# A MoE decoder layer in fp32: experts' rows gathered from an fp32 copy, and a scatter among the last down products

## What is computed

```python
logits = (xt @ router_w + router_b)
top_val, top_idx = lax.top_k(logits, 4)
gates = softmax(top_val)
# for each expert e, over the rows xb of its tokens with gates wb:
gu = xb @ w_gate_up[e] + b_gate_up[e]          # 1024 -> 2048
g, u = gu[:, :1024], gu[:, 1024:]
g = min(g, 7); u = clip(u, -7, 7)
act = (u + 1) * (g * sigmoid(1.702 * g))
ys = (act @ w_down[e] + b_down[e]) * wb        # 1024 -> 1024
# summed back into the tokens' rows, plus the residual
```

## Time and profile before

| | |
|---|---|
| median of 3 runs | 1109.57 us |
| profiled execution | 1112.72 us |
| its span | 1110.9 us |
| PE (matmul) busy | 1056.3 us, 95% |
| DVE, ACT busy | 282.3 us, 157.9 us |
| HBM read | 430.82 MB, 389 GB/s over the span |
| mean granted TensorE clock | 0.985 of full |

### The profile page before, as it was taken

How to read it: one execution, slowest core, us unless ns; L and a number is a source line. 1 busy time by engine, 2 the same in 40 slices (tenths; PEclk the granted TensorE clock), 3 DMA queues, 4 the chain that set the end, 5 groups by cost and what they waited for, 6 DMA issues and landing times.

```text
span 1110.9 us, 14806 instructions
## 1 busy us (share of the span) xinstructions
PE 1056.3 (95%) x6243; PEld 489.1 (44%) x6243; DVE 282.3 (25%) x719; ACT 157.9 (14%) x325; POOL 29.8 (3%) x32
## 2 busy tenths in 40 slices
PE   9999999999999999979999979899798898999998
PEld 7788885543333333333333333333233333333333
DVE  2599843531111111111111111111011111111131
ACT  3453351410000000000000000000000000000011
POOL 1000053000000000000000000000000000000000
PEclk9999999999999999999999989999899999999999
DMA  9933289799999999999999999999999999999997
GB/s 299 316 109 115 93 278 411 279 422 437 428 429 436 428 434 434 431 434 434 434 439 422 441 437 425 437 424 445 432 432 434 425 439 424 432 428 432 424 421 290
DMA packets 43593, 432.25 MB, mean 389 GB/s; under 512 B 3987, under 2 KB 22750, under 8 KB 29262
## 3 DMA queue, kind: packets, MB, share of 16 engines
q1 hardware_dynamic: 43246, 431.77, 93.2%
q10 hardware_dynamic: 160, 0.07, 0.0%
q0 software_dynamic: 160, 0.04, 0.0%
HBM read 430.82 MB, written 1.05 MB: 389 GB/s over the span
## 4 chain that ended last, share of the span: by engine, by line
PE 71%; DMA 27%; ACT 1%; issue 1%; SPq 0%; DVE 0%; POOL 0%; DVEq 0%; ACTq 0%; POOLq 0%
PE psum L1035 30%; DMA arena<-in_w_gate_up 25%; PE psum L1077 14%; PE psum L804 5%; PE psum L677 3%; PE psum L980 3%; PE psum L860 3%; PE psum L1087 3%; PE psum L887 2%; DMA arena<-in_w_down 2%; PE psum L1051 1%; PE psum L987 1%; ACT arena L1470 1%; PE psum L1056 1%; PE psum L788 1%
## 5 line engine op out<-in xcount | busy, mean ns | idle before, releaser
L1035 PE MATMUL psum<-arena 128*64 128x512 f32 x2016 | 455.4, 610 | 37.5 <-DMA arena<-in_w_gate_up 28.9
L1035 PEld LDWEIGHTS psum<-arena 128*64 128x64 f32 x2016 | 151.9, 140 | 334.9 <-issue 306.5
L1077 PE MATMUL psum<-arena 128*64 128x512 f32 x960 | 211.1, 592 | 0.0
L1806 DVE TENSOR_SCALAR arena<-psum 128x512 f32<-128x512 f32 x32 | 22.2, 692 | 704.1 <-PE psum L1035 693.9
L1077 PEld LDWEIGHTS psum<-arena 128*64 128x64 f32 x960 | 67.0, 137 | 124.1 <-issue 121.3
L1457 ACT COPY arena<-psum 128x256 f32<-128x256 f32 x32 | 12.0, 374 | 547.3 <-PE psum L987 547.3
L1087 PE MATMUL psum<-arena 64*128 64x512 f32 x248 | 61.6, 614 | 7.6 <-ACT arena L1470 7.6
L804 PE MATMUL psum<-arena 128*128 128x256 f32 x256 | 59.1, 380 | 0.3 <-ACT arena L1345 0.3
L1470 ACT COPY arena<-psum 128x512 f32<-128x512 f32 x31 | 18.2, 587 | 238.0 <-PE psum L1077 236.5
L804 PEld LDWEIGHTS psum<-arena 128*128 128x128 f32 x256 | 47.6, 190 | 7.9 <-issue 1.2
L980 PE MATMUL psum<-arena 128*128 128x64 bf16 x1488 | 48.8, 191 | 2.2
(11 more groups left out here) (257 smaller groups left out, 604.8 us busy)
## 6 DMA issues: line engine op xcount, KB each, us to landing
arena<-in_w_down SPq DMA_DIRECT2D x26, 4096.0 KB, 30.9
arena<-in_w_gate_up SPq DMA_DIRECT2D x18, 4096.0 KB, 32.7
arena<-in_w_gate_up SPq DMA_DIRECT2D x19, 2048.0 KB, 34.3
arena<-in_w_gate_up SPq DMA_DIRECT2D x14, 1024.0 KB, 11.6
arena<-in_w_down SPq DMA_DIRECT2D x6, 2048.0 KB, 12.9
arena<-in_w_in SPq DMA_DIRECT2D x9, 1024.0 KB, 6.3
arena<-in_w_down SPq DMA_DIRECT2D x9, 1024.0 KB, 21.2
arena<-in_w_in SPq DMA_DIRECT2D x8, 512.0 KB, 8.7
```

The lines of the kernel that those rows point to most:

```text
L1035: last = mm(b[64 * half:64 * half + 64, :], xe[i][:, k, :], channels(w, half), start=(k == 0 and first), stop=(k == KD - 1 and last_stops))
L1077: last = mm(b[64 * c:64 * c + 64, :], aT[:, j, 64 * h:64 * h + 64], slot_dn[slot][:, j, c * 512:(c + 1) * 512], start=False, stop=(h == DC ...
L1806: ts(g_s, G, LIMIT, None, ALU.min).then_inc(S.g_ready, 1)
```

## The change

The three bf16 parts are gone. In their place `xn`, an fp32 copy of the normed state with its channels in the experts' order, is laid out once, in eight pieces by ScalarE (`rows_part`); DVE's part in it falls away, and TensorE and DVE wait for it by one count (`rows_ready`). `ph` becomes fp32; two of its three buffers move to the words of the router's weights, which are no longer needed by then. The gather is 8 x 2 fp32 products, each piece of channels over two token halves, in place of 48 bf16 ones. Apart from that, in the tail, the scatter of expert 30 moves from ahead of the last expert's down products to behind the first half of the down's first piece.

```diff
@@ -306,12 +306,9 @@
         ph_first = grid(at, 2, SLOTS); at += 2 * SLOTS
         tk = words(at, 512); at += 512
 
-        def half_words(at):
-
-            return words(at, 64).bitcast(BF16).rearrange("p (t s) -> p t s", t=2)
-
         wp = [grid(at, 2, P), grid(WB + 5248, 2, P), grid(at + 256, 2, P)]; at += 512
-        ph = [half_words(at), half_words(WB + 5120), half_words(at + 64)]; at += 128
+        ph = [grid(at, 2, SLOTS)] + [rwt.rearrange("p k e -> p (k e)")[:, 2 * SLOTS * i:2 * SLOTS * (i + 1)].rearrange(
+            "p (t s) -> p t s", t=2) for i in range(2)]; at += 128
         pick = [words(at + 32 * i, 32).bitcast(BF16) for i in range(ROUND - 1)] + [words(WB + 5184, 32).bitcast(BF16)]; at += 128
         xe = [grid(at, KD, SLOTS), grid(WB + 5504, KD, SLOTS), grid(at + 512, KD, SLOTS)]; at += 1024
         sT = [grid(at, 2, P), grid(WB + 6016, 2, P), grid(at + 256, 2, P)]; at += 512
@@ -323,8 +320,7 @@
         PARTS = 3 * E
         staged = words(slot_at[3], 3 * D)
 
-        xn3 = words(WB, 3072).bitcast(BF16).rearrange("p (t s d) -> p t s d", t=2, s=3)
-        remains = xe[0].rearrange("p k s -> p (k s)").rearrange("p (b n) -> p b n", b=2)
+        xn = words(WB, 2 * D).rearrange("p (t j q) -> p t j q", t=2, j=KD)
         at = WB + 3072
         first_up = words(WB + 5248, FF)
         g_s = words(at, 512); at += 512
@@ -381,7 +377,7 @@
                      "lnsum_ready lncent_ready lnsq_ready lnvar_ready lnroot_ready lny_ready silu_ready ymix_ready mix_ready "
                      "h1_ready ssq_ready rest_ready h1root_ready hT_ready hT_last "
                      "router_ready logits_ready bound_ready exp_done mask_ready rank_ready place_ready "
-                     "hi_ready remains_ready mid_ready split_ready cnt_ready counted seeded gathered_mid gate_ready overflow_ready bias_step used built gathered "
+                     "rows_ready cnt_ready counted seeded gathered_mid gate_ready overflow_ready bias_step used built gathered "
                      "part_used xe_half xe_ready turned sT_ready g_ready a_step sg_ready act_ready aT_done aT_ready y_ready scattered0 scattered "
                      "down_half tail_step fin_act fin_dve stored").split():
             sem(name)
@@ -976,9 +972,8 @@
                 pe.wait_ge(S.sT_ready, n)
                 for k in range(KD):
                     for t in range(2):
-                        for part in range(3):
-                            last = mm(X[:, k * SLOTS:(k + 1) * SLOTS], xn3[:, t, part, k * P:(k + 1) * P],
-                                      ph[i][:, t, :], start=(t == 0 and part == 0), stop=(t == 1 and part == 2))
+                        last = mm(X[:, k * SLOTS:(k + 1) * SLOTS], xn[:, t, k, :], ph[i][:, t, :], start=(t == 0),
+                                  stop=(t == 1))
                 last.then_inc(S.gathered, 1)
 
             def turn(n, i):
@@ -1163,7 +1158,7 @@
                     pe.wait_ge(S.bias_step, BIAS_STEPS)
                     last = biases(0, ROUND - 1, False)
                 last.then_inc(S.used, 1)
-            pe.wait_ge(S.split_ready, 2 * GC)
+            pe.wait_ge(S.rows_ready, 2 * GC)
             gather(1, SIDE[0])
             biases(1, 0, True)
             pe.wait_ge(S.seeded, 4)
@@ -1206,9 +1201,10 @@
                 last = down_fine(1, down_piece(E - 2, 1), j)
             last.then_inc(S.used, 1)
             pe.wait_ge(S.aT_ready, E)
-            scatter(E - 2, SIDE[-1])
             for h in range(DC):
                 for j in range(DR):
+                    if h == 0 and j == DR // 2:
+                        scatter(E - 2, SIDE[-1])
                     first = last_down(h, j, 0)
                     last = last_down(h, j, 1)
                 if h == DC - 1:
@@ -1426,30 +1422,22 @@
                 y = tk[:, E * t:E * (t + 1)]
                 f(y, y, ACT.Exp, bias=tk[:, 124 + t:125 + t]).then_inc(S.exp_done, 1)
 
-            def high_part(m):
+            def rows_part(m):
                 t, c = m // GC, m % GC
-                f(xn3[:, t, 0, 256 * c:256 * (c + 1)].rearrange("p (j q) -> p j q", j=GR), h1_rows(t, c), ACT.Copy,
-                  scale=rsh[:, t:t + 1]
-                  ).then_inc(S.hi_ready, 1)
-
-            def middle_part(m):
-                t, c = m // GC, m % GC
-                act.wait_ge(S.remains_ready, m + 1)
-                nc.scalar.copy(xn3[:, t, 1, 256 * c:256 * (c + 1)], remains[:, m % 2, :]).then_inc(S.mid_ready, 1)
+                f(xn[:, t, GR * c:GR * (c + 1), :], h1_rows(t, c), ACT.Copy, scale=rsh[:, t:t + 1]
+                  ).then_inc(S.rows_ready, 1)
 
             act.wait_ge(S.logits_ready, 2)
-            high_part(0)
-            high_part(1)
+            rows_part(0)
+            rows_part(1)
             for t in range(2):
                 for c in range(2):
                     n = 384 if t and c else 512
                     if t and c:
                         act.wait_ge(S.gathered_mid, 1)
                     nc.scalar.copy(psum[:, 2 * t + c, 0:n], h1[:, t, 512 * c:512 * c + n]).then_inc(S.seeded, 1)
-            for m in range(2 * GC):
-                middle_part(m)
-                if m + 2 < 2 * GC:
-                    high_part(m + 2)
+            for m in range(2, 2 * GC):
+                rows_part(m)
             X, Y = psum[:, 6, :], psum[:, 7, :]
 
             def turned_out(n, i):
@@ -1850,27 +1838,7 @@
             dve.wait_ge(S.gathered, 1)
             rows_out(first, 2 * GR, KD, natural, psum[:, 7, :]).then_inc(S.xe_ready, 1)
 
-            def remains_of(m):
-                t, c = m // GC, m % GC
-                dve.wait_ge(S.hi_ready, m + 1)
-                if m >= 2:
-                    dve.wait_ge(S.split_ready, m - 1)
-                stt(remains[:, m % 2, :].rearrange("p (j q) -> p j q", j=GR),
-                    h1_rows(t, c), rsh[:, t:t + 1],
-                    xn3[:, t, 0, 256 * c:256 * (c + 1)].rearrange("p (j q) -> p j q", j=GR), ALU.mult, ALU.subtract
-                    ).then_inc(S.remains_ready, 1)
-
-            def low_part(m):
-                t, c = m // GC, m % GC
-                dve.wait_ge(S.mid_ready, m + 1)
-                tt(xn3[:, t, 2, 256 * c:256 * (c + 1)], remains[:, m % 2, :], xn3[:, t, 1, 256 * c:256 * (c + 1)],
-                   ALU.subtract).then_inc(S.split_ready, 1)
-
-            remains_of(0)
-            for m in range(2 * GC):
-                if m + 1 < 2 * GC:
-                    remains_of(m + 1)
-                low_part(m)
+            dve.wait_ge(S.rows_ready, 2 * GC)
             activations(0, GC, SIDE[0], first=True)
 
             with dve.Fori(0, (E - 2) // ROUND) as it:
```

## The result

| | before | after |
|---|---|---|
| median | 1109.57 us (1107.26 to 1111.09, 5 runs) | 1129.11 us (1126.02 to 1130.11, 5 runs) |
| ratio | | 1.0168, 95% interval [1.0145, 1.0192] |
| profiled execution, its span | 1112.72, 1110.9 us | 1129.24, 1127.4 us |
| mean granted clock | 0.985 | 1.0 |

The change makes the kernel 1.7% slower, 19.5 us in the medians and 16.5 us in the profiled spans. The forecast was 1123.7 us in a range of 1115 to 1131. (The median of the kernel before is that of 5 runs, not 3.)

A forecast was written before the change was run, and what follows sets the result against it. DMA sets the end now, with 52 us of TensorE slack; 31 gathers x 2.01 add 62 us, 48 absorbed by waits and low clock. Span 1125.0, 14.1 more, added to the 1109.57 median: 1123.7 us, range 1115 to 1131.

The forecast's parts named there:

- step: One expert's turn of the loop on TensorE: 26.26 us before, 28.27 forecast, 2.01 more for the gather.
- expert 7's load: Early in the loop: its four weight pieces issued 12 us later, at 369.6, landing at 391.0, 8.5 later.
- step 26: Late in the loop: waits for its weights, beginning at 943.6 against 935.12; TensorE alone would begin it at 937.4.
- last piece of down: Tail: the weight stream's last load, landing at 1111.4 against 1102.9, with TensorE reaching it only near 1117.
- the slack: Experts' loop: TensorE's 30 steps took 839.8 us where 787.8 would do, 52 us of slack.
- the ring's lead: Weight slots, full when the loop begins: slower steps free them later, so loads land 8.5 us later.
- the waits at low clock: Experts' loop: TensorE's waits for gate and up weights, some followed by granted clock 0.50, would be almost gone.
- A: Rival, whole loop: the stream hides a cheap gather (1.7 us), so no change, 1109.6 us; chance 0.07.
- C: Rival, loop start: freed DVE and ScalarE let loop and first loads start earlier, cheap gather, about 1105 us; chance 0.03.
- B: Rival, gather: weight loads don't overlap at all, 0.19 us each, 6.1 us a gather, 1202 us; chance 0.02.
- D: Rival, loop: the stream pauses repeatedly because slots come free late, 1 us in a third of steps, 1134 us; chance 0.08.
- the stream: DMA's expert weight loads: 29.08 us an expert, unbroken from expert 7's load, expert 26's landing at 943.5.

The follow-up runs named there:

- e8: The changed kernel with only 64 of each piece's 128 channels held in the gather: 1111.41 us against 1111.08 for the kernel before, ratio 1.0002.
- e6: The changed kernel with the scatter of expert 30 put back ahead of the last down products: 1130.37 us, 1.2 over the changed kernel.
- e9: The changed kernel with only 32 of the 64 slots moving in the gather: 1156.10 us, ratio 1.0403 to the kernel before.
- e1: The kernel before with 16 useless bf16 matmuls ahead of each gather: 1127.89 us against 1108.40, ratio 1.0162.
- e4: The changed kernel with the gather's products for one half of the tokens only: 1114.59 us against 1108.40 for the kernel before, ratio 1.0046.
- f1: The changed kernel with half the tokens' gather and 4 fp32 products of 512 columns ahead of it: 1175.82 us against 1110.86 before, ratio 1.0584.

## Why the prediction was right, point by point

| step of the sum | forecast | measured |
|---|---|---|
| gather in the chain | 3.58 us | 3.75 |
| step | 28.27 | 28.45 |
| first step begins | 230.66 | 229.24 |
| expert 7's load issued, landed | 369.6, 391.0 | 369.10, 391.05 |
| step 26 begins | 943.6 | 945.11 |
| loop ends | 1085.0 | 1085.43 + 1.99 = 1087.42 |
| from there to the last scatter | 33.2 | 33.12 |
| last piece of down lands | 1111.4 | 1112.17 |
| span | 1125.0 | 1127.4 |
| time | 1123.7 | 1129.11 |

The mechanism held in each step: more time of TensorE than the slack, the ring's lead lost early, the waits at low clock gone, nobody waiting for the last piece. The size came out low: 14.1 us of rise were forecast, 16.5 measured in the spans and 19.5 in the medians. Rivals A and C asked for a cheap gather, which the real one is not. e8 made one, and got A's time (no change, 1111.41 against 1111.08) and not C's gain. B, loads that don't overlap, would have given 6.1 us. D didn't come: the DMA share is 0.99 to 1.01 in each 100 us from 400 to 1000.

What was mis-sized:

- The gather, by 0.17 us. The records do start every 0.112 us, as line 951 said, but I multiplied by 32 and left out the hand-over at the end: the old 1.57 was a measured whole, with its edge, and the new 3.58 a pure count. 31 x 0.17 would be 5 us, but up to step 26 the stream sets the time and hides it. Of the 2.4 us that the span is over the forecast, 0.9 are the last five steps at 28.45 in place of 28.27, and 1.5 are the stream's, by which step 26 begins later.
- The first step came 1.4 us early: gate and up of the first expert took 3.65 us for its first 16 records where it had taken 5.35 (208.41 in the trace of before, at a granted clock of 0.91 from 208 to 228 us). That is not the change's doing: e6 has the changed kernel's code up to there and took 5.58 us.
- The stream from expert 7 to 19 took 741.43 - 391.05 = 350.4 us, 1.4 more than 12 x 29.08. The sum had it unbroken. The whole difference lies at its start: expert 8's load, issued at 397.51, landed 24.1 us later, some 30.5 behind expert 7's, while the DMA share was 0.68 from 376 to 380 us and 0.72 from 388 to 392. From there on an expert's load lands every 29.1 us.
- The last 3 us are in how the profiled execution was tied to the median. I took off 3.1 us, as the profiled run of before lay above its median; the one of after lies on it. Runs of either kernel spread by 4 us, and one execution's place in that spread doesn't carry over.
- Two of the steps from which the range was made don't follow from the forecast's own model. At 0.129 us a record TensorE alone would set the end, at 231.2 + 30 x 28.81 = 1095.5 for the loop, 10.5 us over the sum and not 14; at 0.107 the stream still sets step 26, and the sum falls by some 2 us and not 4. And the wait at step 26 is 943.6 - 937.4 = 6.2, not 5.9. With half of 10.5 in place of half of 14 the range would have ended at 1129.0, so that 1129.11 lies within it owes something to luck.

## What to carry to other kernels

When two resources are both busy all the time, compare their times per step, find which one waits for the other, and price a change against the slack of the whole loop. Here that is 52 us, 1.7 a step, and a rise of 2.2 a step went from hidden to deciding. It is not the 2.8 us between the two paces, 26.26 and 29.08: the loop begins with a full ring, so the stream has less to move in it than TensorE has to do. For a held operand of 128 columns and few moving ones, the held side sets the price (e8, e9), so an fp32 product (two records at 0.112 us) costs more than three bf16 ones (0.033 each). A filler for an experiment has to be small in instructions as well as right in time, and its form has to be priced from a row of the same form.

## What the runs showed of the hardware that I had not expected

- 160 more instructions in a loop of some 1640 made TensorE load its code in each turn: 64 packets in place of 18, and waits of up to 7.06 us, each followed by slower products, after the first at clock 0.50 (e1).
- The branch over the unused pass at the end of the program took 3.84 us in one kernel and 0.35 in another (e4).
- TensorE's clock fell behind 3.7 us of back-to-back records with 32 moving columns, 0.54 over the next 3.5 us, with 0.08 us of idle time ahead of it, and not with 64 (e9).
- An fp32 record of 512 columns took 0.46 us with 128 columns held (3.67 for 8, f1), and 0.217 in the pairs of 64 held columns that write the two halves of a bank.
